# In each beat of attention the next head's scores ahead of values, weights and turn, on all engines

## What is computed

```python
s = einsum('bshd,bmhd->bhsm', q, k) * HEAD_DIM ** -0.5
p = softmax(where(mask, s, -inf))
o = einsum('bhsm,bmhd->bshd', p, v)
```

```python
sc = einsum('bqhmd,bkhmd->bhmqk', qblk, k) * scale
p = softmax(where(allowed, sc, -inf))
w = p[:, :, 0] - lam_full * p[:, :, 1]
out = einsum('bhqk,bkhe->bqhe', w, v)
```

## The kernel before

| step (block 1 / layer) | PE | DVE | ACT |
|---|---|---|---|
| `score1` / `dscore` | scores (L1067 / L1208), once the mask of u - 1 is done | scale and mask into `sm` (L2152, L2154 / L2485), row peak (L2141) | exponentials into `ex` with row sums (L1585 / L1748), once the peak is there |
| `weigh1` / `dweigh` | none | reciprocal and weights in `ex` (L2160 to L2164 / L2494 to L2499), once the exponentials are done | none |
| `turn1` / `dturn` | transposes (L1080 / L1219), once weighed | none | copy into `wt` (L1593 / L1757) |
| `out1` / `dout` | values (L1095 / L1234), once turned and copied | low parts, block 1 only | two copies (L1598) / copy and square with sum (L1764, L1766) |

## Time and profile before

### The profile page before, as it was taken

How to read it: one execution, slowest core, us unless ns; L and a number is a source line. 1 busy time by engine, 2 the same in 40 slices (tenths; PEclk the granted TensorE clock), 3 DMA queues, 4 the chain that set the end, 5 groups by cost and what they waited for, 6 DMA issues and landing times.

```text
span 2030.5 us, 35295 instructions
## 1 busy us (share of the span) xinstructions
PE 2002.8 (99%) x14178; PEld 1826.7 (90%) x14178; DVE 1392.0 (69%) x2079; ACT 1095.3 (54%) x1761; POOL 146.5 (7%) x150
## 2 busy tenths in 40 slices
PE   8999999999999999999999999999999999999998
PEld 6889899899988889998999989998888989899996
DVE  7866688745556777678775556556578677886555
ACT  6677466534443667658544443433468756753442
POOL 1200000000000001720000000000000380000000
PEclk9999999999999999999999999999999999999999
DMA  7434456545754444553645754575344554464563
GB/s 276 161 126 145 156 187 211 203 137 187 254 174 147 166 144 142 187 171 125 228 134 187 249 176 146 186 254 185 131 166 142 161 184 155 146 208 146 186 208 123
DMA packets 273003, 355.23 MB, mean 175 GB/s; under 512 B 10203, under 2 KB 226029, under 8 KB 272877
## 3 DMA queue, kind: packets, MB, share of 16 engines
q1 hardware_dynamic: 271533, 349.23, 51.2%
q0 software_dynamic: 1344, 4.23, 0.8%
HBM read 352.35 MB, written 1.08 MB: 174 GB/s over the span
## 4 chain that ended last, share of the span: by engine, by line
PE 89%; DVE 6%; ACT 3%; issue 2%; POOL 1%; DMA 0%; DVEq 0%; ACTq 0%; POOLq 0%
PE ps L798 24%; PE ps L800 17%; PE ps L807 17%; PE ps L808 7%; PE ps L802 7%; PE ps L792 4%; PE ps L794 4%; PE ps L793 4%; DVE ring_r L1881 2%; PE ps L1277 1%; PE ps L1023 1%; POOL small L2630 1%; ACT ring_hi L1400 1%; PE ps L1208 1%; DVE conv_s L2376 1%
## 5 line engine op out<-in xcount | busy, mean ns | idle before, releaser
L1881 DVE TENSOR_TENSOR ring_r<-ring,ring_hi 128x1024 fp32r<-128x1024 f32 x602 | 732.6, 1224 | 417.7 <-ACT ring_hi L1400 416.4
L1400 ACT ACTIVATE ring_hi<-ring 128x1024 fp32r<-128x1024 f32 x602 | 632.6, 1059 | 595.1 <-PE ps L807 364.6
L798 PE MATMUL ps<-xT_hi,ring_hi 128*128 128x256 f32 x2784 | 682.2, 284 | 1.7 <-issue 1.7
L800 PE MATMUL ps<-xT_r,ring_hi 128*128 128x256 f32 x2784 | 672.5, 280 | 0.0
L798 PEld LDWEIGHTS ps<-xT_hi,ring_hi 128*128 128x128 f32 x2784 | 524.7, 188 | 16.8 <-issue 12.1
L800 PEld LDWEIGHTS ps<-xT_r,ring_hi 128*128 128x128 f32 x2784 | 524.8, 189 | 0.0
L807 PE MATMUL ps<-xT_hi,ring_r 128*128 128x256 f32 x2784 | 384.9, 280 | 0.0
L807 PEld LDWEIGHTS ps<-xT_hi,ring_r 128*128 128x128 f32 x2784 | 353.1, 188 | 0.0
L2630 POOL TENSOR_TENSOR small<-small,const 128x1 f32<-128x1 f32 (+3 forms) x32 | 38.0, 1187 | 1841.5 <-DVE small L2305 1268.5
L802 PE MATMUL ps<-ring_hi,tok_r 128*128 128x512 f32 x344 | 135.7, 395 | 0.0
L798 PE MATMUL ps<-ring_hi,xT_hi 128*128 128x512 f32 x312 | 125.4, 402 | 2.6 <-issue 2.6
(11 more groups left out here) (374 smaller groups left out, 2881.8 us busy)
## 6 DMA issues: line engine op xcount, KB each, us to landing
ring<-in_w_mix_in SPq DMA_DIRECT2D x88, 1024.0 KB, 5.0
ring<-in_ffn_w_in SPq DMA_DIRECT2D x80, 1024.0 KB, 5.0
ring<-in_ffn_w_out SPq DMA_DIRECT2D x44, 1024.0 KB, 4.8
ring<-in_w_branch SPq DMA_DIRECT2D x24, 1024.0 KB, 5.1
ring<-in_w_in SPq DMA_DIRECT2D x22, 1024.0 KB, 5.0
ring<-in_w_ffn_up SPq DMA_DIRECT2D x22, 1024.0 KB, 5.0
ring<-in_w_ffn_down SPq DMA_DIRECT2D x11, 1024.0 KB, 4.9
ring<-in_w_mix_out SPq DMA_DIRECT2D x8, 1024.0 KB, 5.9
```

The source lines that it names most:

```text
L798: pe.matmul(out_, stat[0], mov[0], start=first, stop=False)
L800: pe.matmul(out_, stat[0], mov[1], start=False, stop=False)
L1400: act.activation(half_of(high_of(s), s, q), half_of(ring[:, s % SLOTS, :], s, q), ACT.Copy).then_inc(w_hi, 1)
L1881: return dve.tensor_tensor(lo, whole, hi.bitcast(F32), ALU.subtract)
```

## The change

In both tables of beats the score step moves from the last place to the first. The lags go with the steps, so that each beat still holds the scores of unit i, the values of i - 3, the weights of i - 1 and the turn of i - 2.

```diff
-    beats = beats_of(2 * PAIRS, ("out1", "weigh1", "turn1", "score1"), (3, 1, 2, 0))
+    beats = beats_of(2 * PAIRS, ("score1", "out1", "weigh1", "turn1"), (0, 3, 1, 2))
...
-    beats += beats_of(2 * DH, ("dout", "dweigh", "dturn", "dscore"), (3, 1, 2, 0))
+    beats += beats_of(2 * DH, ("dscore", "dout", "dweigh", "dturn"), (0, 3, 1, 2))
```

## The result

The changed kernel takes 2063.9 us (median of 4 runs, 2062.75 to 2065.0); the kernel before, run beside it, takes 2034.25 us (2032.64 to 2035.18). The ratio is 1.0151, with an interval of 1.0139 to 1.0164: 29.65 us slower, where 31.6 were forecast. The profiled execution has a span of 2061.0 us.

The account below looks back on a forecast made before the run. PE bounds the kernel now; the new order closes a longer DVE-ACT round that becomes the bound. Two layers +27.6 and block 1 +4.0 add 31.6 to 2034.75, giving 2066 us, range 2050 to 2079.

Parts of the forecast that it names:

- the closed round: Attention beats: mask, peak, exponentials, ACT copies, split, low split, next mask; wide and narrow total 9.46 us against PE's 8.12.
- Its length: Round in the layers, summed from single rows: 5.11 us for a wide beat, 4.35 for a narrow one.
- the wide round of block 1: Block 1's round for a 256-key beat, with copies of values of 0.35 us: 5.04 us.
- A layer: Each layer's attention: mask-to-mask sum 78.6 us against 66.8, plus 2.0 behind the last score, +13.8 in all.
- the tail: Behind the last score, values of two beats wait for turn's copy: +2.0 us a layer, 1.6 in block 1.
- The convolution beats: Layer beats with DVE's convolution taps or extra products of the xbc chunk: mask distances of 10.8, 5.7 and 4.95 us.
- Block 1: Block 1's attention: rounds sum to 69.6 us against 67.2, plus 1.6 behind the last score, +4.0 in all.
- PE's saving: Scores first on PE: 0.19 us a beat in block 1, 3.8 in all, hidden inside PE's new waits.
- The 0.05 a beat for the layers: PE's saving in the layers, put between 0 and 0.19 us a beat, 26 times: 1.3 us.
- The clock, a rival that came true in small: PE's clock falls to 1.2 GHz in half of the attention stretches: 60 to 100 us more, 2130; chance 0.03.

Follow-up runs that it names:

- split_ahead: The changed kernel, but ACT's weight split stands at the head of the beat, ahead of the exponentials: 2034.43 us, ratio 1.0007 to the kernel before.
- low_split_late: The changed kernel, but DVE's low split stands behind the next beat's mask and peak: 2050.62 us, ratio 1.0080 to the kernel before.
- turn_copy_ahead: The changed kernel, but on ACT turn's copy stands ahead of the weight split: 2072.31 us, ratio 1.0195 to the kernel before.
- both_open: The changed kernel with DVE's low split behind the next mask and peak, and ACT's turn copy ahead of the split: 2041.84 us, ratio 1.0036 to before.
- pe_only: The kernel before, with only PE in the new order: 2032.0 us, ratio 0.9995.
- pe_dve: The kernel before, with PE and DVE in the new order and ACT in the old: 2031.24 us, ratio 0.9989; again 2031.08 us, ratio 0.9992.
- layers_only: The changed kernel with block 1's table of before, so the new order in the two layers alone: 2058.73 us, ratio 1.0128 to the kernel before.

## Why the prediction was right

**The bound.** It named the closed round as what would take PE's place as the bound. split_ahead, which opens it on ACT, takes the loss away; low_split_late, which opens it on DVE, takes 13 of the 29.65 us; turn_copy_ahead, which makes it longer, costs more, though it brings forward what PE waits for; both_open turns the sign of that edit. No theory of a single engine's order gives all four.

**Its length.** 5.07 and 4.32 in the layers against 5.11 and 4.35; 5.0 for the wide round of block 1 against 5.04. The sum of the links, read from single rows before, held within 0.06 us in all four kinds of round; the hand-overs of a closed round cost no more than those of an open one.

**A layer.** From first to last mask 78.4 us, forecast 78.6. The first layer grew by 12.8 and the second by 13.4, forecast 13.8: the over-count is in the tail (what the stage has beyond its first to last mask grew from 10.0 to 11.5 us, by 1.5 where I had put 2.0) and in the rounds. I gave the 78.6 also as the distance of the scores, which was loose: PE runs ahead of the last mask, and from first to last scores it is 76.6.

**The convolution beats.** The distance there, forecast 10.8, 5.7 and 4.95, was 10.65, 5.66 and 4.93.

**Block 1.** +3.3 in the stage and +3.6 in the total, forecast 4.0. From first to last mask it is 69.0 us where I had summed 69.6, as each round is some 0.05 shorter than my sum. I held that sum against 67.2, which runs to the last single matmul of the scores; from mask to mask it was 67.1 before, so the growth is 1.9. The tail grew by 1.4, where I had put 1.6. From first to last scores it is 67.9, which I had also given as 69.6.

**PE's saving.** 0.19 in a beat of block 1 was 0.20, and was off the path, as said: it shows in pe_only, pe_dve, split_ahead and both_open (-3.0 us, of which 13 beats of 0.20 are 2.6; the rest has no row), not in the whole change. That a change of array mode drains the engine (the Trainium skill, TensorEngine Tiling (Array Packing), Key Properties) agrees with this price; that it is the draining that costs the 0.20 is not shown by a row. The 0.05 a beat for the layers was not seen: with PE's and DVE's order alone the layers are 76.98 and 77.01 against 77.06 and 77.05, where 13 such beats would give 0.65. That term of the sum had no row behind it, and counting the changes of form would have put it at nothing: in a layer only the scores leave the `128*128` form, so there are two changes in a beat in either order. It changed nothing, since it lay inside the waits.

**The clock, a rival that came true in small.** I held the clock's fall for a rival of 100 us with a chance of 0.03, since waits of 0.69 left the clock at 1.00. In the changed kernel PE waits 1.69 us for a mask and, after 0.49 of scores, 2.89 for turn's copy, and comes back at half pace. Three stretches, then PE's time line:

```profile
750.00:754.00 4.00, 0.49 (x4) 0.33 (x4) 2.60 (x8) 2.11 (x8) 0.00 (x0) 1.00 0.81 262
754.00:758.00 4.00, 3.33 (x16) 3.33 (x17) 3.52 (x8) 3.37 (x11) 0.00 (x0) 0.60 0.01 3
758.00:762.00 4.00, 4.00 (x32) 3.54 (x32) 2.70 (x5) 1.44 (x5) 0.00 (x0) 0.97 0.01 4
```

```profile
751.28 0.49 PE L1208 MATMUL ps<-kT,qT 64*128 64x128 f32 x4 [1.69 <-DVE sm L2485]
754.67 1.12 PE L1234 MATMUL ps<-tok,wt 128*128 128x128 f32 x4 [2.89 <-ACT wt L1757]
...
756.44 0.41 PE L800 MATMUL ps<-xT_r,ring_hi 128*128 128x256 f32 x1
756.65 0.42 PE L798 MATMUL ps<-xT_hi,ring_hi 128*128 128x256 f32 x1
...
758.43 0.28 PE L800 MATMUL ps<-xT_r,ring_hi 128*128 128x256 f32 x1
758.55 0.28 PE L798 MATMUL ps<-xT_hi,ring_hi 128*128 128x256 f32 x1
```

Matmuls start 0.21 us apart up to 758.15 and 0.12 apart behind it: the 1.2 GHz level, then the 2.4 GHz level again. From 754.67 to 758.15 that is some 1.7 us of PE's time in a layer. In the first layer none of it reached the end, as the masks kept the distances of the sum: the round was the bound there too. In the second it did. There PE comes back at 1564.83 and stays at half pace until about 1570.9, some 3 us of its time, and the mask of unit 7 has to wait for its scores:

```profile
1564.00:1571.00 7.00, 6.17 (x29) 6.07 (x29) 5.10 (x10) 4.97 (x14) 0.00 (x0) 0.53 0.03 8
...
1571.78 0.69 DVE L2485 SCALAR_TENSOR_TENSOR sm<-ps,const 128x512 f32<-128x512 f32 x1 [0.50 <-PE ps L1208]
```

Its distance is 5.50 in place of 4.93, which is the 0.6 us by which the second layer is longer than the first. In layers_only, with the same code in the layers, PE comes back at half pace as well, for some 4.6 and 3.4 us, no mask waits there, and the layers are equal (89.94 and 89.91). Where the round is open the fall lies on the path: in low_split_late PE is at 0.50 and 0.58 of its clock behind waits of 2.00 and 2.89 us, and the distance from the mask of unit 6 to that of unit 7 is 8.10 us in place of the 4.43 of before (the one ahead of it is 2.77 in place of 4.11, so the two together grew by 2.3):

```profile
750.00:752.00 2.00, 1.41 (x6) 1.42 (x7) 1.68 (x5) 1.94 (x5) 0.00 (x0) 0.50 0.00 0
752.00:754.00 2.00, 2.00 (x12) 2.00 (x11) 1.14 (x3) 2.00 (x9) 0.00 (x0) 0.50 0.00 0
754.00:756.00 2.00, 2.00 (x12) 2.00 (x12) 0.00 (x0) 0.67 (x2) 0.00 (x0) 0.58 0.04 8
```

The clock has a share in this: 750.59 to some 755.7 at half pace is 2.6 us of PE's time. How much of it is in the distances was not isolated. Pauses of PE after which it comes back at half pace are what the Trainium skill, TensorE: Matmul & The Clock Gate, HAM oscillation, describes. In the changed kernel this came once in a layer, and not at the waits of 1.24.

## What to carry to other kernels

When a change moves steps of in-order engines, follow what each queue's last step of a beat waits for and what its first one of the next beat waits behind: if the path comes back to where it began, the time once round, summed link by link from single rows of the profile of before, is a new bound on the beat, and it is to be held against the busiest engine's beat. The step that the busiest engine waits for in the trace after is where it meets the round, not what makes it long: an edit has to take a link out of the round (here the split ahead of the exponentials), and one that only serves the named wait may cost time until that is done. Reorder engines one by one before all together: here PE's and DVE's new orders are harmless or a little better, and ACT's undoes them.

## What was not expected of the hardware

The same wait lowered the clock in one layer and not in the other. In split_ahead PE waits 1.95 us for turn's copy at the convolutions of each layer. The two waits, and the stretch behind each with its granted clock, first layer and then second:

```profile
745.05 0.71 PE L1264 MATMUL ps<-tok,wt 128*128 128x128 f32 x4 [1.95 <-ACT wt L1787]
...
745.00:748.00 3.00, 2.95 (x25) 2.95 (x26) 2.67 (x9) 2.94 (x6) 0.00 (x0) 1.00 0.78 273
```

```profile
1544.46 0.71 PE L1264 MATMUL ps<-tok,wt 128*128 128x128 f32 x4 [1.95 <-ACT wt L1787]
...
1545.00:1549.00 4.00, 4.00 (x23) 4.00 (x22) 3.68 (x9) 3.52 (x11) 0.00 (x0) 0.57 0.44 152
```

The code of the two layers is the same and before they take 77.06 and 77.05 us; here they take 77.90 and 79.43. The 1.5 us between them is what this one fall cost where the round is open, and the nearest thing to a price of it in this study; the half pace from about 1545.6 to 1549.0 is 1.7 us of PE's time. In both_open, with waits of 2.04 and 1.95 us 0.49 us of scores apart, the clock fell as well:

```profile
744.98 0.49 PE L1260 MATMUL ps<-kT,qT 64*128 64x128 f32 x4 [2.04 <-DVE sm L2537]
747.42 1.22 PE L1286 MATMUL ps<-tok,wt 128*128 128x128 f32 x4 [1.95 <-ACT wt L1809]
...
748.00:752.00 4.00, 4.00 (x21) 4.00 (x20) 2.81 (x6) 3.94 (x13) 0.00 (x0) 0.50 0.00 0
```

So the clock can fall after one pause of 1.95 us, where I had held it safe from anything but a long run of waits; what decides it was not found. The stages outside attention also moved by up to 5.3 us in all between executions of kernels with the same code there (the last column of the table), with no cause found.
